# Gate and up units: high and low activation rows side by side in 512-column matmuls, halves added afterwards

## The reference

```
def swiglu(h, w_in, w_out):          # h 256x1024, w_in 1024x5632, w_out 2816x1024
    gu = h @ w_in
    g, u = jnp.split(gu, 2, axis=-1)
    return (jax.nn.silu(g) * u) @ w_out
```

## Time and profile before

| | |
|---|---|
| time before, median of 3 runs | 1620.56 us (1616.83 to 1620.96) |
| the profiled execution: its time, its span | 1617.68 us, 1615.9 us |
| TensorE matmul, weight load | 87%, 82% of the span |
| VectorE, ScalarE, GpSimd | 79%, 38%, 21% |
| mean granted TensorE clock | 0.931 of full speed |
| HBM | 306 MB read, 190 GB/s over the span |

### The profile page before, as it was taken

One profiled execution on the slowest core, in us unless ns is written; L12 is line 12 of the kernel. 1 busy time (PEld: TensorE's weight loads), 2 busy tenths in 40 slices (PEclk: granted clock), 3 DMA queues, 4 the chain that ended last, 5 costly groups with the idle time before them and its releaser, 6 DMA issues.

```text
span 1615.9 us, 27634 instructions
## 1 busy us (share of the span) xinstructions
PE 1409.8 (87%) x10570; PEld 1323.9 (82%) x10570; DVE 1269.9 (79%) x1719; ACT 620.3 (38%) x933; POOL 344.2 (21%) x322
## 2 busy tenths in 40 slices
PE   3899997899999799999758999999879757866897
PEld 2899997899998599999648999999758536754796
DVE  6898777987878888787765787756776999999574
ACT  3343334433335443334534433346436311322343
POOL 7992000000000100000100000000640478776000
PEclk8799999999999999999978999999979878987999
DMA  9688874587763668785204777654403112212352
GB/s 371 224 300 300 296 288 172 191 328 298 273 221 118 241 229 311 274 301 191 79 26 170 272 276 277 229 165 138 161 27 118 64 53 79 67 64 78 126 177 64
DMA packets 65357, 308.57 MB, mean 191 GB/s; under 512 B 7264, under 2 KB 8576, under 8 KB 59008
## 3 DMA queue, kind: packets, MB, share of 16 engines
q1 hardware_dynamic: 65280, 307.52, 53.4%
HBM read 306.44 MB, written 1.05 MB: 190 GB/s over the span
## 4 chain that ended last, share of the span: by engine, by line
PE 68%; DVE 24%; issue 3%; ACT 3%; POOL 1%; DMA 0%; DVEq 0%; ACTq 0%; POOLq 0%
PE tiles L325 14%; PE tiles L327 14%; PE tiles L326 14%; PE acc L325 5%; PE acc L326 5%; PE acc L327 5%; DVE arena L1463 4%; DVE w_lo L317 4%; PE mods L414 2%; DVE arena L1110 2%; PE acc L567 2%; PE nrm L424 1%; PE tiles L447 1%; DVE arena L1459 1%; ACT w_hi L313 1%
## 5 line engine op out<-in xcount | busy, mean ns | idle before, releaser
L317 DVE TENSOR_TENSOR w_lo<-land,w_hi 128x1024 fp32r<-128x1024 f32 x391 | 491.6, 1263 | 196.8 <-ACT w_hi L313 195.1
L313 ACT CAST w_hi<-land 128x1024 fp32r<-128x1024 f32 x391 | 408.3, 1045 | 574.2 <-PE tiles L327 360.8
L325 PE MATMUL tiles<-x_hi,w_hi 128*128 128x256 f32 x1512 | 436.4, 289 | 13.6 <-DVE w_lo L317 6.9
L326 PE MATMUL tiles<-x_lo,w_hi 128*128 128x256 f32 x1512 | 430.2, 285 | 0.0
L327 PE MATMUL tiles<-x_hi,w_lo 128*128 128x256 f32 x1512 | 429.9, 284 | 0.0
L325 PEld LDWEIGHTS tiles<-x_hi,w_hi 128*128 128x128 f32 x1512 | 292.4, 193 | 23.0 <-issue 14.3
L326 PEld LDWEIGHTS tiles<-x_lo,w_hi 128*128 128x128 f32 x1512 | 292.4, 193 | 1.9 <-issue 1.9
L327 PEld LDWEIGHTS tiles<-x_hi,w_lo 128*128 128x128 f32 x1512 | 292.4, 193 | 0.0
L325 PE MATMUL tiles<-a_hi,w_hi 128*128 128x256 f32 (+1 forms) x720 | 211.2, 293 | 25.4 <-DVE arena L1489 20.7
L1110 DVE SCALAR_TENSOR_TENSOR arena<-arena,csil 128x512 f32<-128x512 f32 x280 | 215.1, 768 | 2.0
L327 PE MATMUL tiles<-a_hi,w_lo 128*128 128x256 f32 (+1 forms) x720 | 208.2, 289 | 0.0
(11 more groups left out here) (250 smaller groups left out, 1919.0 us busy)
## 6 DMA issues: line engine op xcount, KB each, us to landing
land<-in_stream SPq DMA_DIRECT2D x391, 512.0 KB, 4.0
arena<-in_gstream SPq DMA_DIRECT2D x46, 2048.0 KB, 8.4
x<-in_x_t SPq DMA_DIRECT2D x1, 1024.0 KB, 14.3
arena<-in_ssm_c SPq DMA_DIRECT2D x1, 1024.0 KB, 6.7
arena<-in_ssm_b SPq DMA_DIRECT2D x1, 1024.0 KB, 4.8
out_t<-x SPq DMA_DIRECT2D x8, 128.0 KB, 1.9
cons<-in_cons SPq DMA_DIRECT2D x1, 624.5 KB, 9.0
arena<-in_band SPq DMA_DIRECT2D x1, 544.0 KB, 13.1
```

Of the source, the lines that this page charges most:

```text
L313: nc.scalar.copy(w_hi[:, u % RING], land[:, u % LAND]).then_inc(hi_done, 1)
L317: nc.vector.tensor_tensor(w_lo[:, u % RING], land[:, u % LAND], w_hi[:, u % RING].bitcast(F32), ALU.subtract).then_inc(lo_done, 1)
L325: nc.tensor.matmul(outs, lh, rh, start=first, stop=False, **kw)
L326: nc.tensor.matmul(outs, lh, rl, start=False, stop=False, **kw)
```

## The change

The activations' high and low rows are stored side by side (`x_parts`, `a_parts`), and a gate or up unit takes, for each of its 8 weight tiles, one matmul of 512 columns (high weight by high and low rows) and one of 256 (low weight by high rows, into the first half). The gate product now fills bank 0 and the up product bank 1, and both are two halves that have to be added. ScalarE copies the second half of each bank to SBUF, VectorE adds the first half to it from PSUM. ScalarE takes over the rounding of the hidden tile (`hidden_hi`). Gate j has to wait for the add of gate j-1, up j for the add of up j-1. Tile 0 and the out units keep their 256-column matmuls; `first_units` only writes its low products into the second half.

More of the change, by code:

```diff
@@ L437, in column_unit, with first_units @@
                 m.then_inc(used, 1)
-            def first_units(u, outs, hi, lo, before, one_bank=False):
+            def first_units(u, outs, hi, lo, before, lows=None):
                 for c in range(2):
@@ L446, in first_units @@
                         lh, ll = w_tile(u + c, k * P, P)
-                        nc.tensor.matmul(outs[c], lh, hi[:, k], start=(k == 0 and not (c and one_bank)), stop=False,
+                        nc.tensor.matmul(outs[c], lh, hi[:, k], start=(k == 0), stop=False,
                                          skip_group_check=True)
@@ L453, in first_units @@
                             pe.wait_ge(xl_done, before + k + 1)
-                        m = nc.tensor.matmul(outs[c], w_tile(u + c, k * P, P)[0], lo[:, k], start=False,
+                        m = nc.tensor.matmul((lows or outs)[c], w_tile(u + c, k * P, P)[0], lo[:, k], start=False,
                                              stop=(k == KT - 1), skip_group_check=True)
@@ L500, in out_unit, with ffn @@
                 m.then_inc(used, 1)
-            def ffn(f, stage, hi=x_hi, lo=x_lo):
+            def ffn(f, stage, parts=x_parts):
                 base, o0, b = FFN_BASE[f], TILE[f"ffn{f}"], G_FFN[f]
-                nd = OWNER[:o0].count("d")
                 wait_bank(pe, o0)
-                first_units(base, [tiles[:, 0, 0:T], tiles[:, 0, T:2 * T]], hi, lo, KT * stage, one_bank=True)
                 wait_bank(pe, o0 + 1)
-                gate_unit(base, 1, g_unit(base, 1), 0, hi, lo)
-                up_unit(1, g_unit(base, 1) + 1, 0, hi, lo)
+                first_units(base, [tiles[:, c, 0:T] for c in range(2)], parts[:, :, 0], parts[:, :, 1], KT * stage,
+                            [tiles[:, c, T:2 * T] for c in range(2)])
+                gate_unit(f, 1, g_unit(base, 1), 0, parts)
+                up_unit(f, 1, g_unit(base, 1) + 1, 0, parts)
                 if f == 2:
@@ L852, in ffn @@
                         for m in range(4):
[L853 to L856 removed]
+                            j, u = j0 + m, g_unit(base, j0 + m)
+                            split_hi(act, u, i)
[5 more added lines that the diff above has]
+                            hidden_hi(f, j - 1, i, 4)
                     j0 += 4 * reps
+                gate_copy(f, 21, 0)
                 split_hi(act, o_unit(base, 21))
[L859 removed]
+                up_copy(f, 21, 0)
+                silu_step(f, 21, 0, 0)
+                hidden_hi(f, 21, 0, 0)
             def head_square(n, src):
```

58 lines of the change are left out of this document (25 added, 33 removed).

## The result

| | before | after |
|---|---|---|
| time, median of 17 runs each | 1618.97 us (1615.82 to 1620.96) | 1622.15 us (1618.72 to 1626.71) |
| ratio | | 1.0024, interval 1.0015 to 1.0033 |
| profiled execution, span | 1615.9 us | 1619.5 us |
| mean granted TensorE clock | 0.931 | 0.929 |

A forecast was written before the change was run, and what follows sets the result against it. TensorE was taken to bound the blocks' insides, VectorE hidden. 17.9 - 7.6 - 1.5 - 1.0 - 1.1 = 6.7 us gained gave 1611.0 us from the profiled execution, 1613.9 from the median; forecast 1612 us, range 1603 to 1620.

The forecast's parts named there:

- a pair costs 227 + 120 = 347 ns: Gate and up units: one 512-column and one 256-column matmul take 347 ns, against 360 for three narrow ones.
- The term of 17.9 us: Saving from the wide matmul: 1344 pairs in four blocks, 13.3 ns each, bounds 0 and 35.8 us.
- the sum of 6.7 us gained: Whole kernel: 17.9 us saved less costs of 7.6, 1.5, 1.0 and 1.1 us.
- Rival (c): Gate and up units: a pair keeps its 360 ns, gain 0, costs 11.2 us, 1629 us in all; chance 0.07.
- The estimated 1625 us: Whole-kernel time if a warm matmul's fixed cost is about 2.5 ns and the wide matmul saves only 3.4 us.
- The starts: Block starts: gate 2 later by 2.6 us in block 0, 2.05 in blocks 1 and 2; sum 7.6 us lost, bounds 4 and 10.
- The clock: Starts of blocks 1 and 2: TensorE's clock may fall in the longer gap before gate 2; 1.5 us lost, bounds 0 and 4.6.
- Inside a block: VectorE's tile grows from 7.2 to 7.7 us and stays hidden under TensorE's 8.87 us; new waits cost nothing.
- rival (d): All tiles: VectorE becomes the bound at 9.3 us a tile, 1640 us in all; chance 0.05.
- The 1.0 us for GpSimd's stretch: Block 0, seven tiles: GpSimd slows VectorE's multiplication, now with two SBUF inputs; 1.0 us lost, bounds 0 and 2.5.
- The ends: Block ends: update about 1.1 us later; costs 0.1 us each in blocks 1 and 2, 0.9 in block 3; sum 1.1.
- Ahead of the blocks: Up to out 0: gate 1 and up 1 gain 0.85 us, against block 3's 0.25 us wait.

The follow-up runs named there:

- three narrow: Changed kernel with gate and up units back to three 256-column matmuls per weight tile, the rest of the change kept: 1626.25 us, ratio 1.0046 to the kernel before.
- groups of eight: Changed kernel with each gate or up unit's eight wide matmuls first, then its eight narrow ones: 1614.57 us, ratio 0.9972 to the kernel before.
- reversed: Changed kernel with a unit's eight wide matmuls first, in reversed weight-tile order (7 to 0), then its eight narrow ones: 1617.34 us in one run.
- fours: Changed kernel with a unit's 16 matmuls as four wide, four narrow, four wide, four narrow: 1614.94 us in one run.
- the end: Changed kernel with the last tile's rounding back on VectorE, ahead of ScalarE's splits: 1621.07 us, ratio 1.0016 to the kernel before.
- GpSimd later: Changed kernel with GpSimd's 512-element table products of block 0 waiting for gate 2: 1619.99 us, ratio 1.0006 to the kernel before.
- the kernel before with GpSimd later: Kernel before the change, with only GpSimd's 512-element table products of block 0 made to wait for gate 2: 1616.30 us, ratio 0.9988.
- gain of the starts: Changed kernel with ScalarE's fifth split before tile 0's up copy, VectorE rounding tile 0, and the loop's gate add ahead of split and part: 1612.02 us, ratio 0.9963.

## Why the prediction was wrong

**The step that failed** is "a pair costs 227 + 120 = 347 ns". The mechanism was right, one cost per matmul and not per column, and both pure streams have it: 120.0 and 226.6 ns come back behind the fifth wide and the second narrow matmul of a group. But the change never runs a pure stream. Two widths in turn cost 6.4 ns a pair more, half of the 13.3 ns that were to be saved. The term of 17.9 us measured 84 x 0.104, some 8.8 us, well inside its bounds of 0 and 35.8; with it the sum of 6.7 us gained becomes 2.4 us lost, so this step alone turns the sign of the forecast. In the sum I took the middle with the argument that "both pure streams show the same extra", which says nothing about the alternation. Rival (c), that a stream of both widths keeps its 360 ns, was half true and had a chance of 0.07. The kernels with eight, four and one in a group, and the one with three narrow matmuls, show the cause. The 2.5 ns of fixed cost that the Trainium skill states ("TensorE: Matmul & The Clock Gate", section "Wait — 56ns, not 53.3ns?") fits none of the spacings here (120.0 and 226.6 against 106.7 and 213.3 ns of columns). The estimated 1625 us by it lies nearer to the measured 1622 than my 1612, but by luck, since its size of the cost is not the one in the rows.

**The starts** were right in kind and a little small: 8.8 us against 8.0. Block 1, +1.88 us, was forecast at 2.05. In block 0 I took 1.3 us for the later start of the parts and stretched only the last part and the add for GpSimd, 1.3 us more. That stretch did not come: from the reduction to gate 2 it is 2.00 us, against 1.99 before. The eight parts themselves, shifted against GpSimd's products, grew instead, from 0.48 + 7.73 to 1.28 + 9.30 us: +3.65 in all. The seven of them before:

```profile
57.38 7.73 DVE L1110 SCALAR_TENSOR_TENSOR arena<-arena,csil 128x512 f32<-128x512 f32 x7
```

**The clock** fell in the new gap of block 2. I had 1.5 us in the sum for all blocks, and this one cost about that much. That block 1 kept its full clock in the changed kernel's profiled execution was luck. Six of the later kernels start their blocks in the changed kernel's order (three narrow, groups of eight, reversed, fours, the end, GpSimd later), and it fell there in all six: 13.53 and 13.59 us from out 0 to out 1 at a mean of 0.87, and 14.67 to 14.74 at 0.77, against the 12.35 at 1.00.

**Inside a block** VectorE stayed hidden, as its waits said: from 140 to 240 us it is busy 84.7 us, some 7.6 us of a tile's 8.97 (forecast 7.7), and rival (d) is out. The 1.0 us for GpSimd's stretch was not there: tiles 3 to 8 take 8.60 and 9.34 like all others, although the multiplication went from 419 to 649 ns beside GpSimd.

```profile
L1162 DVE TENSOR_TENSOR arena<-arena 128x256 f32<-128x256 f32 x7 | 4.5, 649 | 0.0
```

**The ends**: blocks 1 and 2 +0.02 each (forecast 0.1), block 3 +0.71 (0.9). Block 0 was costed at nothing and took 0.97. Behind its update VectorE has coefficients, a split and several parts to do before the reciprocal, without a wait between, so the update's delay goes straight to the norm.

**Ahead of the blocks** 0.6 us were to be gained and 1.5 were lost. 0.85 of it is block 2's. That goes with the clock and needs no change of code: from its first matmul to gate 1 it took 15.46 us at a mean granted clock of 0.78 before, 16.34 at 0.69 after, and 16.22 at 0.68 in the kernel before with GpSimd later, which has no edit there. In blocks 1 to 3 the gain of gate 1 and up 1 did not show: from gate 1 to out 0 it is 5.75 us, against 5.76 before.

**What stays open.** The stretches outside the blocks have the same instructions in every kernel and still took from 736.5 to 742.8 us in the 13 profiled executions. So a total moves by some 4 us through them, and the whole-kernel gain of the starts (10 us for 5.5), of the groups of eight (7.6 us for 5.2 in the tiles) or of the three narrow matmuls is not wholly their own. Whether they move with what stands ahead of them or from run to run, one profile of each kernel can't tell. What the change of width does inside TensorE no run here shows.

## What to carry to other kernels

A price read from a stream of equal instructions holds for such a stream. When a change mixes two kinds, bound the mix, and keep instructions of one width together: the same matmuls in groups of eight gave 5.2 us in 76 tiles here, 0.3%, for an edit of a few lines. Where a stage starts with a serial chain over three engines, the order of the first few instructions on each can be worth more than half of what the steady state gives: 5.5 us in three starts, against 8.8 us in 84 tiles. An engine that slows another (GpSimd here) has to be moved to where that other engine has time, not just away. And one profile of a kernel can hold a clock that the next one does not: a start is priced from several.

## What the runs showed of the hardware

In the four-byte type used here, with a weight load for each matmul, a stream of one width runs at 120.0 (256 columns) and 226.6 ns (512 columns) per matmul at full clock. After eight or more narrow matmuls the next five wide ones take 233, 236, 228, 233 and 231 ns, the same to a nanosecond in 34 units, gate and up alike, and whatever the weight tile; the first narrow ones behind eight wide take 113 and 119. After only four narrow ones the series is another (235, 233.5, 235.9, 224). A VectorE operation over two SBUF tensors of 512 columns took 0.75 us alone, and up to 1.78 us beside GpSimd's products. After a gap of 1.7 us at the reduction the granted clock of block 1 stayed at 1.00 in the changed kernel and was 0.50 in the one with GpSimd later; where it fell, the start took 2.4 us more.
